# Down projections of a two-layer transformer block: seven of 22 chunk pairs folded instead of six, with four and two plain chunks between them in turn, and another order of the splits

## The reference, cut to what matters

```python
D_MODEL, SEQ, D_FF = 2048, 256, 5632

def conv_ffn(h, w_gate, w_up, conv_w, conv_b, w_down):
    a = causal_dwconv(h @ w_gate, conv_w, conv_b)
    return (jax.nn.silu(a) * (h @ w_up)) @ w_down      # [256, 5632] @ [5632, 2048]

def reference(x, norm_g, ...):
    for i in range(2):
        ...                                            # norm, attention, norm
        h = rmsnorm(x, g[2])
        x = x + rmsnorm(conv_ffn(h, ...), g[3])
    return x
```

## Time and profile before

| what | value |
|---|---|
| median of three runs | 2100.68 us |
| the profiled execution | 2100.99 us, of which the span is 2099.3 us |
| PE busy | 2089.9 us, 100% of the span, 12113 matmuls |
| DVE busy | 1504.4 us, 72% |
| ACT busy | 1113.8 us, 53% |
| line L968 (plain chunks of the down projections) | 1464 matmuls in two groups, 395 ns each |
| folded pairs | 24, six in each of the four pairs of units |

### The profile page before, as it was taken

How to read it: one execution, slowest core, us unless ns; L and a number is a source line. 1 busy time by engine, 2 the same in 40 slices (tenths; PEclk the granted TensorE clock), 3 DMA queues, 4 the chain that set the end, 5 groups by cost and what they waited for, 6 DMA issues and landing times.

```text
span 2099.3 us, 34382 instructions
## 1 busy us (share of the span) xinstructions
PE 2089.9 (100%) x12113; PEld 1791.6 (85%) x12113; DVE 1504.4 (72%) x2348; ACT 1113.8 (53%) x1703; POOL 287.0 (14%) x462
## 2 busy tenths in 40 slices
PE   9999999999999999999999999999999999999999
PEld 9997888888888888888999987888888888888887
DVE  7655676776676778888876655576776776788887
ACT  6675564444444455555666776454444444455454
POOL 4452000000000000000065773000000000000000
PEclk9999999999999999999999999999999999999999
DMA  7444456555555555554673333455555555555554
GB/s 257 145 154 166 160 189 200 183 182 197 181 180 199 180 200 209 193 199 157 236 252 121 102 111 131 153 191 197 180 190 191 179 190 194 179 205 208 196 190 141
DMA packets 111013, 381.46 MB, mean 182 GB/s; under 512 B 14194, under 2 KB 18754, under 8 KB 110402
## 3 DMA queue, kind: packets, MB, share of 16 engines
q1 hardware_dynamic: 108466, 373.63, 51.9%
q10 hardware_dynamic: 2448, 6.53, 0.9%
HBM read 377.97 MB, written 2.14 MB: 181 GB/s over the span
## 4 chain that ended last, share of the span: by engine, by line
PE 96%; DVE 2%; DMA 1%; ACT 1%; issue 0%; ACTq 0%; SPq 0%; DVEq 0%
PE set L862 32%; PE set L866 16%; PE set L968 14%; PE set L1240 11%; PE set L940 8%; PE set L980 2%; PE set L982 2%; PE set L981 2%; PE set L1314 2%; PE set L1082 1%; PE set L1288 1%; PE set L1336 1%; DMA raw<-in_stream 1%; PE set L1114 1%; PE set L1290 1%; PE set L1338 0%
## 5 line engine op out<-in xcount | busy, mean ns | idle before, releaser
L2071 DVE TENSOR_TENSOR wlo<-raw,whi 128x1024 fp32r<-128x1024 f32 x655 | 799.3, 1234 | 354.3 <-ACT whi L1563 351.9
L1563 ACT ACTIVATE whi<-raw 128x1024 fp32r<-128x1024 f32 x655 | 683.8, 1055 | 549.1 <-PE set L866 351.4
L862 PE MATMUL set<-hs,whi 128*128 128x512 f32 x2896 | 953.1, 395 | 0.6 <-DVE wlo L2271 0.3
L866 PE MATMUL set<-hs,wlo 128*128 128x256 f32 x2896 | 682.1, 281 | 0.0
L866 PEld LDWEIGHTS set<-hs,wlo 128*128 128x128 f32 x2896 | 534.8, 188 | 60.1 <-DVE wlo L2071 0.4
L862 PEld LDWEIGHTS set<-hs,whi 128*128 128x128 f32 x2896 | 497.4, 189 | 69.8 <-issue 1.4
L968 PE MATMUL set<-whi,hid 128*128 128x512 f32 x976 | 273.4, 395 | 0.0
L968 PEld LDWEIGHTS set<-whi,hid 128*128 128x128 f32 x976 | 183.1, 188 | 45.3 <-DVE wlo L2071 0.6
L1240 PE MATMUL set<-hs,whi 128*128 128x256 f32 x1280 | 213.2, 286 | 0.1
L1240 PEld LDWEIGHTS set<-hs,whi 128*128 128x128 f32 x1280 | 176.6, 189 | 2.7 <-issue 0.9
L845 POOL COPY cw<-conv_sb 128x16 f32 x20 | 41.9, 2096 | 848.7 <-DVE gate L2770 848.7
(11 more groups left out here) (274 smaller groups left out, 2106.1 us busy)
## 6 DMA issues: line engine op xcount, KB each, us to landing
raw<-in_stream SPq DMA_DIRECT2D x703, 512.0 KB, 3.9
gain_rows<-rows ACTq DMA_DIRECT2D x4, 1024.0 KB, 5.2
xT<-in_x SPq DMA_DIRECT2D x8, 256.0 KB, 7.6
out_y<-out_f SPq DMA_DIRECT2D x8, 256.0 KB, 2.4
bo_rows<-rows ACTq DMA_DIRECT2D x1, 768.0 KB, 9.8
wg_raw<-in_w_gates ACTq DMA_DIRECT2D x1, 768.0 KB, 4.7
raw<-in_stream SPq DMA_DIRECT2D x2, 256.0 KB, 4.3
bo_last<-rows ACTq DMA_DIRECT2D x1, 256.0 KB, 11.9
```

The lines of the kernel that those rows point to most:

```text
L862: return mm(sets[set_of(u)][:, t, 0:2 * w], whi[:, slot, cols], r, start=first, stop=final)
L866: return mm(sets[set_of(u)][:, t, w:2 * w], wlo[:, slot, cols], r[:, 0:w], start=False, stop=False)
L1563: A(whi[:, slot, :], raw[:, slot, :], ACT.Copy).then_inc(hi_ready, 1)
L2071: V.tensor_tensor(wlo[:, slot, :], raw[:, slot, :], whi[:, slot, :].bitcast(F32), ALU.subtract).then_inc(lo_ready, 1)
```

## The change

`FOLDED` has seven indices instead of six. Between the folds stood four plain chunks each time; now `BETWEEN_FOLDS` puts four, two, four, two, four, two there. On ACT and DVE the two parts that split the ring blocks are moved into the functions `ring_high` and `ring_low`. `ring_leads(n)` is true for the first fold of a pair and for a fold that has only two plain chunks ahead of it. For these, ACT runs `ring_high` ahead of the high parts of `fold_h` and `fold_w`, and DVE runs `ring_low` ahead of `fold_h` (for the first fold: behind `fold_h`, ahead of `fold_w`). The other folds keep their order. What the folds compute and the functions of PE and SP are as before; SP and PE follow the new order of chunks.

```diff
-FOLDED = (4, 7, 10, 13, 16, 19)
+FOLDED = (4, 7, 10, 13, 15, 17, 19)
 FOLDS = len(FOLDED)
+BETWEEN_FOLDS = (4, 2, 4, 2, 4, 2)
...
+def ring_leads(n):
+    return n == 0 or BETWEEN_FOLDS[n - 1] == CK
...
@@ ACT, fold_split
-                if n > 0:
+                def ring_high():
+                    act.wait_ge(raw_in[a], 16 * (g // RING + 1))
+                    act.wait_ge(raw_in[b], 16 * ((g + 1) // RING + 1))
+                    act.wait_ge(chunk_used, g - RING + CK)
+                    A(whi[:, b, UNIT:CW], raw[:, b, UNIT:CW], ACT.Copy)
+                    A(whi[:, a, :], raw[:, a, :], ACT.Copy).then_inc(hi_ready, CK)
+                if ring_leads(n):
+                    ring_high()
+                else:
                     split(g - CK)
                     split(g - 1)
...
-                act.wait_ge(raw_in[a], 16 * (g // RING + 1))
-                act.wait_ge(raw_in[b], 16 * ((g + 1) // RING + 1))
-                act.wait_ge(chunk_used, g - RING + CK)
-                A(whi[:, b, UNIT:CW], raw[:, b, UNIT:CW], ACT.Copy)
-                A(whi[:, a, :], raw[:, a, :], ACT.Copy).then_inc(hi_ready, CK)
+                if not ring_leads(n):
+                    ring_high()
...
@@ DVE, fold_split
-                if n > 0:
+                def ring_low():
+                    dve.wait_ge(hi_ready, g + CK)
+                    V.tensor_tensor(wlo[:, b, UNIT:CW], raw[:, b, UNIT:CW], whi[:, b, UNIT:CW].bitcast(F32), ALU.subtract)
+                    V.tensor_tensor(wlo[:, a, :], raw[:, a, :], whi[:, a, :].bitcast(F32), ALU.subtract).then_inc(lo_ready, CK)
+                if n > 0 and ring_leads(n):
+                    ring_low()
+                if not ring_leads(n):
                     split(g - CK)
                     split(g - 1)
...
+                if n == 0:
+                    ring_low()
                 dve.wait_ge(raw_in[a], 16 * (g // RING + 1))
                 dve.wait_ge(raw_in[b], 16 * ((g + 1) // RING + 1))
                 V.tensor_tensor(fold_w[:, 0:2], quarters[:, 2:4], quarters[:, 0:3:2], ALU.subtract).then_inc(fold_w_made, 1)
...
-                dve.wait_ge(hi_ready, g + CK)
-                V.tensor_tensor(wlo[:, b, UNIT:CW], ...)
-                V.tensor_tensor(wlo[:, a, :], ...).then_inc(lo_ready, CK)
+                if not ring_leads(n):
+                    ring_low()
```

More of the change, by code:

```diff
@@ L91 @@
 FIRST_PRODUCTS = 10
-FOLDED = (4, 7, 10, 13, 16, 19)
+FOLDED = (4, 7, 10, 13, 15, 17, 19)
 FOLDS = len(FOLDED)
+BETWEEN_FOLDS = (4, 2, 4, 2, 4, 2)
 PLAIN = [c for c in range(CHF) if c not in FOLDED]
 def down_order(lead):
-    order = [(k, c) for k in range(CK) for c in PLAIN[:lead[k]]]
-    for q, c in enumerate(FOLDED):
+    plain = [iter(PLAIN), iter(PLAIN)]
+    order = [(k, next(plain[k])) for k in range(CK) for _ in range(lead[k])]
+    for c, between in zip(FOLDED, BETWEEN_FOLDS + (0,)):
         order += [(0, c), (1, c)]
-        if q < FOLDS - 1:
-            order += [(k, PLAIN[lead[k] + 2 * q + m]) for m in range(2) for k in range(CK)]
-    return order + [(k, c) for k in range(CK) for c in PLAIN[lead[k] + 2 * (FOLDS - 1):]]
+        order += [(k, next(plain[k])) for _ in range(between // CK) for k in range(CK)]
+    return order + [(k, c) for k in range(CK) for c in plain[k]]
 DOWN_ORDERS = down_order((5, 3)), down_order((4, 2))
@@ L2127, in fold_split @@
                 V.tensor_tensor(fold_w_lo[:, 0:2], fold_w[:, 0:2], fold_w_hi[:, 0:2].bitcast(F32), ALU.subtract).then_inc(fold_w_low, 1)
-                dve.wait_ge(hi_ready, g + CK)
-                V.tensor_tensor(wlo[:, b, UNIT:CW], raw[:, b, UNIT:CW], whi[:, b, UNIT:CW].bitcast(F32), ALU.subtract)
-                V.tensor_tensor(wlo[:, a, :], raw[:, a, :], whi[:, a, :].bitcast(F32), ALU.subtract).then_inc(lo_ready, CK)
+                if not ring_leads(n):
+                    ring_low()
                 dve.wait_ge(fold_w_high, 2 * q + 2)
```

## The result

The changed kernel took 2111.15 us (median of 6 runs, 2109.39 to 2112.86), the kernel before 2100.64 us (6 runs, 2100.48 to 2101.43): a ratio of 1.0049, 95% interval 1.0039 to 1.0060. It is 10.5 us slower. The forecast was 2112.3 us with a range of 2102 to 2119, slower with a chance of 0.83.

The account below looks back on a forecast made before the run. PE, busy all the time, was taken to bound the kernel. Terms -2.79 + 13.2 + 0.3 + 0.6 = +11.3 us on the profiled 2100.99 us gave 2112.3 us, range 2102 to 2119.

Parts of the forecast that it names:

- The saved matmuls: One more folded pair in each of four pairs of units saves 3 PE matmuls each: 2.79 us less.
- The ring: DVE's chain through two fetches in the down projections: 27.65 us against PE's 26.55, losing 13.2 us over 12 rounds.
- a round: One fold behind four plain chunks, one behind two, with six plain chunks: 114 matmuls, 26.55 us of PE.
- two splits: On DVE, the short fold's second half of `fold_w_lo` and the two plain chunks' splits behind it: 3.50 us.
- the first fetch: Fetch into the slot of the long fold's chunk b, behind another fetch: 4.7 us to land, 0.1 until DVE starts.
- the long fold: DVE's work in the fold behind four plain chunks, from `fold_w` to the end of L2130, without a wait: 6.02 us.
- the second fetch: Fetch of the short fold's chunks into slots the long fold frees: 4.65 us, then ACT starts 0.1 later.
- DVE's last step: In the short fold: ring blocks' low parts, `fold_h`, `fold_w` and the first half of `fold_w_lo`, 6.87 us.
- The first rival: Fetches land as on an empty queue, 3.3 us instead of 4.7; PE loses next to nothing in rounds: 2098.8 us, chance 0.11.
- First folds: PE waits 0.45 us at each of four pairs' first folds, 1.8 us, replacing 0.74 at two, 1.48: +0.3.
- shares: At the second pair's end, PE waits some 0.3 us for DVE's last sums, 0.6 in two layers.

Follow-up runs that it names:

- seven folds in the middle order: Changed kernel with the ring blocks split in every fold behind the high and low parts of `fold_h`, ahead of the remaining folded weights: 2097.09 us.
- half fetch: Changed kernel, each down-projection fetch bringing only the first 512 of 1024 columns, 256 KB instead of 512 KB: 2097.99 us, ratio 0.9991.
- doubled sum: Changed kernel with the sum of the hidden halves made a second time on DVE at every fold, into an unread buffer: 2113.68 us, ratio 1.0065.
- six folds in the middle order: Kernel before, its six folds in place, with ring blocks split behind the parts of `fold_h`, ahead of the remaining folded weights: 2099.63 us, ratio 0.9996.
- the old one: Changed kernel's seven folds and distances, but no fold splits its ring blocks first, as in the kernel before: 2110.39 us, ratio 1.0047.

## Why the prediction was right

**The saved matmuls.** 12 x 0.2329 = 2.79 us. The kernels without waits at folds show it: seven folds in the middle order are 2.5 us faster than six.

**The ring.** The prediction put a round at 27.65 us; the twelve rounds have a mean of 27.55, and the loss is 12.0 us instead of 13.2. Step by step in the round shown above, from the second half of `fold_w_lo` at 801.25 on: two splits end at 804.74 (3.49; predicted 3.50); the first fetch, until `fold_w` starts at 809.36, 4.62 (4.88); the long fold up to its ring blocks' low parts, 6.04 (6.02); the second fetch, until ACT starts at 820.19, 4.79 (4.65 + 0.10); ACT, 820.82 + 0.96 - 820.19 = 1.59 (1.58); DVE from 821.80 to 827.62 + 1.14 = 828.76, 6.96 (6.87). The steps on engines were right to 0.1 us. In the twelve rounds they repeat to 0.01 us, but for one of 7.22 in place of 6.96. What moves from round to round (26.96 to 28.21) are the two fetches: the first of these steps took 4.14 to 5.32 us (4.61 in the mean), the second 4.58 to 5.88 (4.84). The half fetch shows that they decide. That the sum came within 0.1 us is in part luck: the first fetch was put 0.27 too long, the second 0.09 and DVE's last step 0.1 too short.

**What stood for the other side.** The first rival, landings as on an empty queue, would have been right with shorter fetches: the half fetch, with 3.0 us instead of 4.2, gave 2097.99 us, and that rival had 2098.8 by its own terms. By the Trainium skill, "DMA: Bandwidth & Descriptors", section "Anatomy of one DMA", whose fit is for DMAs that GpSimd issues, a fetch of 512 KB is an estimate of 3.2 us. Here SP issues them, so the fit is carried over to another path. The twelve fetches from 800 to 830 us had a median of 4.2, and the measurement decides.

**First folds and shares.** 0.45 us at four first folds was 0.38. The waits of before that these replace were 1.37 us and not 1.48, since the second layer's was 0.63. The prediction took it over from the first layer. So the term is +0.15 instead of +0.3. The 0.3 at the shares was 0.35, as in the rows of DVE and PE there, which answer to the earlier trace rows (from start to start 0.50 and then 0.31 us, where 0.233 is the rule):

```profile
983.88 1.28 DVE L2183 TENSOR_TENSOR fold_w_lo<-y,fold_w_hi 128x512 fp32r<-128x512 f32 x2
```

```profile
984.80 0.39 PE L974 MATMUL set<-whi,hid 128*128 128x512 f32 x1
985.30 0.47 PE L1021 MATMUL set<-fold_w_hi,ident_r 128*128 128x512 f32 x1
985.61 0.40 PE L1021 MATMUL set<-fold_w_lo,ident_r 128*128 128x512 f32 x1
```

**What the prediction did not see.** Two things, of which neither moved the number. It charged the first folds only for the wait that stands at them. Their new order also starts the ring 2.25 us late, and that is most of why all twelve rounds lose: with the old order there, some 6.5 us come back. The prediction's twelve full rounds hold only because the ring starts with nothing to spare; its own wait at the first folds implies that, but it does not say so. And it did not ask whether the seventh fold could have been had in the old order. The answer (no, because of the release of `fold_h`) was in its rows: from the first sum of `fold_h` to the end of L2130 it is 785.80 + 1.22 - 780.07 = 6.95 us, more than PE's 6.29.

**What stays open.** How much the doubled sum costs, why the landing of single fetches differs by a microsecond from round to round, and whether the wait in another stage takes the 0.7 us that six folds in the middle order should have saved as well. An eighth fold was not tried.

## What to carry to other kernels

An engine that has only 24.1 us of work in a round of 26.55 can still set the time, if its work hangs in a ring through fetches: go once round, from a release of a buffer to the next release of the same buffer, with what is behind what, and compare that with the bounding engine's time. In such a ring the cheap cure is to move work that needs no fetch into the idle time that the fetch leaves (here 2.41 us became 0.43), and an order is judged by all of its rings: the old one lost 1.03 us a round to a buffer's release, the changed one 1.00 to a fetch, and the one in the middle loses to neither. When undoing one part of a change leaves the time as it is, look at the waits before you call that part harmless.

## What was not expected of the hardware

A fetch of half the bytes from the same rows landed 1.2 us sooner (3.0 against 4.2 us, medians of twelve), a drop of 29% for 50% of the bytes. Landings in the changed kernel's rounds spread so far that rounds of the same instructions took 26.96 to 28.21 us, while the engines' steps repeated to 0.01 us, but for one. The landing of the fetch one split behind another, the first of the two in a round, took 4.02 to 5.20 us, and that of the second fetch of a pair 4.01 to 5.31.
